# Prompt experts of a hybrid decoder step: a ring of 8 slots and sets of 2 in place of 16 and 4, with the query weights of all half heads held in SBUF

## What is computed

```python
def peer_ffn(xn, lp):
    q = (xf @ lp['peer_wq']).reshape(n, PEER_HEADS, 2, PEER_HALF)
    sub = jnp.einsum('nhpd,hpkd->nhpk', q, lp['peer_keys']).astype(jnp.float32)
    top_s, top_i = lax.top_k(sub, PEER_TOPK)
    cand_s = (top_s[:, :, 0, :, None] + top_s[:, :, 1, None, :]).reshape(n, PEER_HEADS, PEER_TOPK * PEER_TOPK)
    ...
    best_s, best_pos = lax.top_k(cand_s, PEER_TOPK)
    idx = jnp.take_along_axis(cand_i, best_pos, axis=-1).reshape(n, PEER_HEADS * PEER_TOPK)
    gate = jax.nn.softmax(best_s, axis=-1).reshape(n, PEER_HEADS * PEER_TOPK).astype(xn.dtype)
    ...
        act = jax.nn.gelu(jnp.einsum('ted,td->te', lp['peer_u'][ib], xb), approximate=False)
        return jnp.einsum('te,ted->td', gb * act, lp['peer_v'][ib])
```

## Time and profile before

| | |
|---|---|
| Runs (3): median, lowest, highest | 4949.02 us, 4946.89 us, 4949.45 us |
| Profiled execution | 4948.49 us |
| Its span, first to last instruction | 4946.3 us |
| PE busy, DVE busy, ACT busy, POOL busy | 81%, 51%, 24%, 29% |
| Bytes moved by DMA | 1267.61 MB, of them 1082.20 MB on POOL's queue |
| Gathers (POOL), mean issue | 1024, 1151 ns |
| Products (DVE), mean | 1024, 1225 ns |
| Mix matmuls (PE), mean | 4096, 645 ns |

### The profile page before, as it was taken

One profiled execution on the slowest core, in us unless ns is written; L12 is line 12 of the kernel. 1 busy time (PEld: TensorE's weight loads), 2 busy tenths in 40 slices (PEclk: granted clock), 3 DMA queues, 4 the chain that ended last, 5 costly groups with the idle time before them and its releaser, 6 DMA issues. The chain is left out here.

```text
span 4946.3 us, 41655 instructions
## 1 busy us (share of the span) xinstructions
PE 4028.2 (81%) x12109; PEld 2091.1 (42%) x12109; DVE 2502.4 (51%) x5470; ACT 1164.1 (24%) x3566; POOL 1411.1 (29%) x1315
## 2 busy tenths in 40 slices
PE   7998688887799998688988778888778887778784
PEld 3555344443456653344444333443334443334331
DVE  2332354553311111378778644877445876446662
ACT  2332122221011011022332222232222322222221
POOL 0000132330000000043433444334444344444441
PEclk9886799888899998789999999999999998899897
DMA  4001000004500103399989999999999999999995
GB/s 177 17 17 49 13 10 17 17 4 131 226 30 34 42 21 137 113 419 418 415 366 419 420 389 421 419 388 419 421 388 419 387 416 421 389 421 419 387 420 212
DMA packets 210803, 1267.61 MB, mean 256 GB/s; under 512 B 23360, under 2 KB 39781, under 8 KB 76176
## 3 DMA queue, kind: packets, MB, share of 16 engines
q0 software_dynamic: 148608, 1082.20, 52.8%
q1 hardware_dynamic: 62024, 183.48, 9.9%
HBM read 1236.03 MB, written 31.63 MB: 256 GB/s over the span
## 5 line engine op out<-in xcount | busy, mean ns | idle before, releaser
L2595 PE MATMUL psum<-ex_ring,ex_diag 128*128 128x512 f32 x4096 | 1996.0, 645 | 508.9 <-ACT ex_diag L2660 508.2
L2788 DVE CUSTOM_DVE_ANT_0 ex_ring<-ex_ring,ex_x_rows 128x1024 f32<-128x1024 f32 x1024 | 1235.4, 1225 | 882.9 <-DMA ex_ring<-in_expert_uv,expert_idx 858.0
L2542 POOL DMA_INDIRECT ex_ring<-in_expert_uv,expert_idx x1024 | 1178.7, 1151 | 1389.1 <-PE psum L2595 1026.6
L2595 PEld LDWEIGHTS psum<-ex_ring,ex_diag 128*128 128x128 f32 x4096 | 826.7, 207 | 1586.1 <-issue 972.6
L2651 ACT ACTIVATE ex_dots<-ex_dots 128x4 f32<-128x4 f32 x256 | 52.6, 205 | 1691.4 <-DVEq L2790 1691.3
L2660 ACT ACTIVATE ex_diag<-ident,ex_weight 128x128 f32<-128x128 f32 x1024 | 327.2, 390 | 18.7 <-issue 1.4
L1041 PE MATMUL psum<-w_zx,ssd_hT 128*128 128x512 f32 (+1 forms) x768 | 297.0, 542 | 3.4 <-issue 1.8
L2574 PE MATMUL psum<-ex_xT,ex_w_q 128*128 128x256 f32 (+1 forms) x1280 | 270.1, 365 | 6.3 <-ACT ex_xT L2623 6.3
L2574 PEld LDWEIGHTS psum<-ex_xT,ex_w_q 128*128 128x128 f32 x1280 | 230.1, 194 | 66.7 <-issue 41.5
L1928 PE MATMUL psum<-w_out,read_mT 128*128 128x512 f32 x512 | 232.9, 605 | 1.7 <-DVEq L2089 0.9
L2655 ACT ACTIVATE ex_weight<-expert_gate,ex_dots 128x1 f32<-128x1 f32 x1024 | 217.7, 283 | 17.9 <-issue 0.3
(11 more groups left out here) (430 smaller groups left out, 3739.2 us busy)
## 6 DMA issues: line engine op xcount, KB each, us to landing
ex_w_q<-in_route_wq SPq DMA_DIRECT2D x80, 512.0 KB, 10.4
ex_ring<-in_expert_uv,expert_idx POOLq DMA_INDIRECT x1024, 26.3
w_zx<-in_w_in SPq DMA_DIRECT2D x1, 10304.0 KB, 29.6
w_out<-in_w_out SPq DMA_DIRECT2D x2, 4096.0 KB
read_mixed<-scratch_mixed SPq DMA_DIRECT2D x8, 1024.0 KB, 4.8
w_out<-in_cache_mem_k SPq DMA_DIRECT2D x8, 1024.0 KB, 11.1
w_qkv<-in_w_in SPq DMA_DIRECT2D x3, 2048.0 KB, 16.0
ex_keys<-in_route_keys SPq DMA_DIRECT2D x80, 64.0 KB, 6.8
```

Source lines behind the costliest of these rows:

```text
L2542: nc.gpsimd.indirect_dma_start(out=ring[:, n % RING, :], out_offset=None, in_=io["expert_uv"], in_offset=bass.IndirectOffsetOnAxis(ap=idx[ ...
L2595: ins = nc.tensor.matmul(psum[2 * (tile % 2) + c][:], diag[:, q % 2, s, :], ring[:, n % RING, D + c * BANK:D + (c + 1) * BANK], start=(n % ...
L2788: nc.vector.tensor_tensor_reduce(ring[:, n % RING, 0:D], ring[:, n % RING, 0:D], x_rows[:, tile % (2 * GT), :], 1.0, 0.0, ALU.mult, ALU.ad ...
```

## The change

The ring has 8 slots, a set 2. The query weights and keys of all 16 half heads lie in SBUF, loaded once at the start of the stage, the keys by one DMA; `looks` and `load_keys` are gone from SP, and PE waits only for the first arrival. SBUF holds about as much as before: 64 KB a partition less ring, 56 KB more weights, 7 KB more keys. On PE and ACT the routing work is spread so that it falls behind the same slots as before, that is at every second set. On DVE a set of products now lies between the two halves, another ahead of `top_of_head`, and the fourth set behind it.

```diff
-    RING = 16
-    SET = 4
+    RING = 8
+    SET = 2
...
-        w_q, keys = sb("ex_w_q", [P, 2, DB, P]), sb("ex_keys", [P, 2, N_KEYS])
+        w_q, keys = sb("ex_w_q", [P, LOOKS, DB, P]), sb("ex_keys", [P, LOOKS, N_KEYS])
...
             def load_w_q(k):
-                if k < (GROUPS + 1) * LOOKS:
-                    if k >= 2:
-                        sp.wait_ge(q_full, k - 1)
-                    i = k % LOOKS
-                    sp.dma_start(w_q[:, k % 2], io["route_wq"][i * P:(i + 1) * P, :].rearrange("p (b n) -> p b n", b=DB)).then_inc(wq_in[k % 2], 16)
...
+                sp.dma_start(w_q[:, k], io["route_wq"][k * P:(k + 1) * P, :].rearrange("p (b n) -> p b n", b=DB)).then_inc(wq_in[k], 16)
...
-            def looks(head):
-                for k in (2 * head, 2 * head + 1):
-                    load_keys(k + 2)
-                    load_w_q(k + 2)
-
             load_x(0)
             load_x(1)
-            for k in range(2):
+            load_w_q(0)
+            sp.dma_start(keys[:], io["route_keys"].rearrange("(k p) n -> p k n", p=P)).then_inc(keys_in, 16)
+            for k in range(1, LOOKS):
                 load_w_q(k)
-                load_keys(k)
             load_x(2)
             load_x(3)
             load_res(0)
             sp.dma_start(gain[:], io["final_norm_w"].broadcast_to([P, D])).then_inc(gain_in, 16)
             load_res(1)
-            for head in range(AHEAD):
-                looks(head)
...
-                if routed_at(step) is not None:
-                    looks(routed_at(step))
...
             def ask(k):
...
-                pe.wait_ge(wq_in[k % 2], 16 * (k // 2 + 1))
+                pe.wait_ge(wq_in[k % LOOKS], 16)
...
                 for i in range(SETS):
-                    if head is not None:
-                        if i % 2 == 0:
-                            ask(2 * head + i // 2)
+                    if head is not None and i % 2 == 0:
+                        if i % 4 == 0:
+                            ask(2 * head + i // 4)
                         else:
-                            score(2 * head + i // 2)
+                            score(2 * head + i // 4)
                     mix(step * SETS + i)
...
                 for i in range(SETS):
                     weights(step * SETS + i)
-                    if head is not None:
-                        if i % 2 == 0:
-                            place_qT(2 * head + i // 2)
+                    if head is not None and i % 2 == 0:
+                        if i % 4 == 0:
+                            place_qT(2 * head + i // 4)
                         else:
-                            place_sub(2 * head + i // 2)
+                            place_sub(2 * head + i // 4)
...
                 if head is not None:
                     top_of_half(2 * head)
-                    top_of_half(2 * head + 1)
                 products(step * SETS + 1)
                 if head is not None:
+                    top_of_half(2 * head + 1)
+                products(step * SETS + 2)
+                if head is not None:
                     top_of_head(head)
+                products(step * SETS + 3)
...
-                for i in range(2, SETS):
+                for i in range(4, SETS):
                     products(step * SETS + i)
```

More of the change, by code:

```diff
@@ L2425, in expert_mix @@
         turned, xT_ready = sem("ex_turned"), sem("ex_xT_ready")
-        wq_in, keys_in = [sem(f"ex_wq_in{i}") for i in range(2)], [sem(f"ex_keys_in{i}") for i in range(2)]
+        wq_in, keys_in = [sem(f"ex_wq_in{i}") for i in range(LOOKS)], sem("ex_keys_in")
         gain_in, count_ready = sem("ex_gain_in"), sem("ex_count_ready")
@@ L2573, in ask @@
                 for b in range(DB):
-                    ins = nc.tensor.matmul(psum[6 + k % 2][:, 0:n], w_q[:, k % 2, b, :], xT[:, b, 0:n], start=(b == 0), stop=(b == DB - 1))
+                    ins = nc.tensor.matmul(psum[6 + k % 2][:, 0:n], w_q[:, k % LOOKS, b, :], xT[:, b, 0:n], start=(b == 0), stop=(b == DB - 1))
                 ins.then_inc(q_full, 1)
@@ L2579, in score @@
                 pe.wait_ge(qT_ready, k + 1)
-                pe.wait_ge(keys_in[k % 2], 16 * (k // 2 + 1))
+                pe.wait_ge(keys_in, 16)
                 for a in range(tiles_of(k // LOOKS)):
-                    ins = nc.tensor.matmul(psum[6 + k % 2][:, N + a * P:N + (a + 1) * P], qT[:, a * P:(a + 1) * P], keys[:, k % 2, :], start=True, stop=True)
+                    ins = nc.tensor.matmul(psum[6 + k % 2][:, N + a * P:N + (a + 1) * P], qT[:, a * P:(a + 1) * P], keys[:, k % LOOKS, :], start=True, stop=True)
                 ins.then_inc(sub_full, 1)
```

## The result

| | before | changed | ratio, 95% interval |
|---|---|---|---|
| Median | 4948.03 us | 5107.79 us | 1.0323 [1.0308, 1.0338] |
| Range, runs | 4946.89 to 4949.45, 4 | 5102.61 to 5113.12, 4 | |
| Span of the profiled execution | 4946.3 us | 5102.0 us | |

The account below looks back on a forecast made before the run. DMA bytes bound the kernel before; in two-tile routed steps a cycle of waits would take over. 90 - 32 + 0 - 4.5 + 15 + 5 = +73.5 us on 4948.49 gave 5022 us, 8-in-10 range 4935 to 5085.

Parts of the forecast that it names:

- the circle that I drew: Routed two-tile steps: waits through share, top_of_head, PE's score and ACT's exponentials close a cycle of 43.9 us before clock loss.
- Rival A: PE's clock is not lost, or where PE has time: a two-tile step takes 43.9 us, total 4935 us; chance 0.11.
- rival B: The cycle does not close and bytes stay the bound in routed steps: -136.5 us, total 4812 us; chance 0.07.
- part 1: The 30 steps routing two tiles: 46.8 us each with clock loss and hand-overs, against 43.8 before, +90 us.
- part 3: Ring of 8 slots: 7.2 us spare per slot turn, so 0 us, with 1.0 us a routed step for the bound.
- part 2: The 8 steps routing sample rows alone: bytes stay the bound, 39.8 us against 43.8, -32 us.
- my +90: The 30 two-tile steps' term: 30 x (46.8 - 43.8) us slower, bounds +3 and +135.
- Rival C: The ring starves the DMA in all steps, the 26 without routing 3.6 us longer each: 5116 us; chance 0.08.
- Start: Start of the expert stage: DVE waits for the gain behind more weight loads, first gather later, +15 us.
- end: End of the stage: the smaller last set is shorter on ACT and PE, -4.5 us.
- first slots: First gathers of the stage: DMA idles 4.8 us that 16 slots hid, +5 us.
- drain: POOL's drain in root, once a tile: the DMA's empty stretch is the same with 8 slots, 0 us.

Follow-up runs that it names:

- e9_warm: The changed kernel with eight added matmuls on PE, output unchanged, in 29 of the 38 routed steps where PE would idle: 5073.64 us, 1.0251 of before.
- e4_ring10: The changed kernel with a ring of 10 slots in place of 8: 4989.80 us, 1.0078 of before.
- the split: The changed kernel with top_of_head cut in two on DVE, its second part behind one more set of products: 4937.77 us, 0.9974 of before.
- e8_no_drain: The changed kernel with the two POOL drains in root replaced by semaphore waits: 5063.59 us, 1.0233 of before.
- e12_before_no_drain: The kernel before with the two POOL drains in root replaced by semaphore waits: 4900.20 us, 0.9903 of before.

## Why the prediction was wrong

**Right: the sign, and what ends the byte bound.** The bytes do leave the path in two-tile steps (DMA share 0.84, forecast 0.85 to 0.9), and waits in a circle take their place, though not the circle that I drew. Rival A (clock not lost) falls by `e9_warm`, rival B (bytes stay the bound) by the DMA share.

**Right: the sum of the cycle, part 1's 46.8.** Where enough slots are there, it is 47.0 and 47.2, the exponentials are the last wait, as drawn, and the clock costs 2.5 us (`e4_ring10`) where I had 2.8. But that is not the changed kernel.

**The step that failed is part 3, "Ring of 8 ... 0", with 1.0 us as its bound.** I compared one slot's turn with its share of the bytes: 12.7 of 19.9 us. That holds where a slot is handed on at once, in steps without routing, and the 24 such steps cost 2.2 us together. For the routed step I wrote that set 3 is 11 us late, that the DMA therefore stops, and that it "has 7 us to spare in a step of 46.8, so this adds little". The spare time exists, but not where it is needed: `share` stands behind two rows of the next step, and these are the third and fourth gathers issued after the stop. The chain from set 3 through the released slot, the landing and the product to `share` competes with the chain through `score` and the exponentials, and it is 3.0 us longer in the step shown. I never summed it. From the rows before it would have read: set 3 on PE 4.3 us behind the head, 3.4 for its first slot at half clock and 1.7 for the second, `ask` 3.45, two more slots 3.4, from issue to product 5.7, a product, share, halves, two sets and head 1.2 + 0.6 + 6.2 + 5.0 + 10.6: 45.6 us, a microsecond from the other chain's 46.8, so no zero. The 3.5 us from there to 49.1 were in no row that I had used. In the step shown they are the fourth gather, issued 3.4 us after PE freed its slot, of which 0.8 us pass at each issue. In 17 of the 30 two-tile steps it is issued 1.7 to 1.8 us behind the third, and then its product comes 7.0 to 8.1 us after the issue and not 5.7, which costs nearly as much. What the missing term measures: two more slots take 98 us out of the 30 two-tile steps (`e4_ring10`: 1390.3 against 1488.5 us) and 10 out of the last nine steps. For want of them the step is 2.3 to 3.4 us longer, where I had put 0 and allowed 1.0 as the bound.

**The same step failed for the sample rows (part 2).** The forecast was 39.8 us a head; it is 42.3, with the ring of 10 or the split 40.7. Of the 22 us that are missing two more slots give back 10 (`e4_ring10`: 369.7 us for the row of 379.7); 12 are missing still.

**What my +90 left out on the other side.** Even where my 46.8 holds, `e4_ring10` has +52 us in the two-tile steps, not +90: the first step behind a stretch without routing takes 40.4 us, since it starts with a full ring, and the eighth and others fall short of 47 too. The median step does not carry a block of eight. So the ring cost 98 us that I had at 0, the cycle 38 less than I had it, and 60 is what is left in the sum. With the 22 us of the sample rows that is 82 of the 86 us between 5022 and 5107.79.

**Rival C** said 5116 us, close to 5107.79, but for another reason: that the slot's turn passes 19.9 us in all steps and lengthens the 26 without routing. Those did not change. It was near in size and wrong in mechanism; that it came so close is luck.

**Right in the small terms.** Start +14.8 (forecast +15), end -4.0 (-4.5), first slots +2.5 (+5, twice too much, but small), drain 0 (within 4 us of that by `e8_no_drain` and `e12_before_no_drain`). The exponentials follow the load of their table at once here too (3328.63 + 1.28 us, then 3329.93), and nothing waits for them; the drain that the Trainium skill gives for a switch of tables (ScalarE: Activation LUTs, What ACT_TABLE_LOAD costs) is not seen in this case.

**Open.** Why POOL issues its fourth gather of the step shown only at 3326.30, 3.4 us after PE freed its slot, with no wait that the profile names, was not looked into. Nor is it shown why, where it follows the third by 1.72 us, its row takes 7.0 to 8.1 us. What keeps the sample rows' steps at 40.7 us with 10 slots wasn't tried apart either.

## What to carry to other kernels

A ring's depth has to be held against the longest stretch in which its consumer is away, not against the mean turn of one slot: sum release, reissue, landing and use as one chain, and compare it with every other chain that ends at the same instruction. When buffers shrink so that traffic can go, cut that longest stretch in two first; here one moved call was worth 170 us, and the 38 MB of traffic only 27 us as long as it was not made (what it is worth behind the split was not tried). A deep ring also banks work between phases, so the slower step of one phase may cost nothing in the sum; a median step doesn't show that, the sum over a phase does.

## What I had not expected of the hardware

- The second of two gathers that start into an idle DMA queue comes late for its bytes. The two of 3315.12 and 3317.15, 2.03 us apart at issue, had their products 3.68 us apart. The third and fourth behind the stop are 1.7 to 1.8 us apart at issue in 17 of the 30 two-tile steps of the change, and their products 2.6 to 4.1, where queued rows come 2.485 us apart. A ring that drains pays this in each step.
- From PE's last matmul of a slot to the issue of the gather into it lie 0.8 us (modelled end 3314.31, gather 3315.12). I had counted 0.1 for all hand-overs of a step.
- A drain on POOL waits for the gathers that stand queued: 27.29 us with 16 slots, 12.10 with 8, and in both the DMA share has fallen to 0.01 or less before it ends. A semaphore between the same two operations costs 0.1 us. Taking it away gave 44 us in the change and 48 in the kernel before.
